# A fused two-block transformer: the second product of gates in the sparse-attention layer moves behind both products of queries

## The reference, cut to what matters

```python
q, kc, vc, ks, vs, kw, vw, gate, z = jnp.split(u @ w_in, points, axis=-1)
q = q.reshape(b, s, G, J, dh) * (dh ** -0.5)
k_cmp = compress(kc, pe_k, w1_k, w2_k)      # 31 compressed positions
v_cmp = compress(vc, pe_v, w1_v, w2_v)
...
s_c = einsum(q, k_cmp) + bias; p_c = softmax(s_c)      # compressed branch
s_s = einsum(q, k_g) + bias;   p_s = softmax(s_s)      # selected branch (all 8 blocks of 8 here)
s_w = einsum(q, k_win) + bias; p_w = softmax(s_w)      # window branch
o = gate[..., 0:1] * o_c + gate[..., 1:2] * o_s + gate[..., 2:3] * o_w
o = o.reshape(b, s, NSA_WIDTH) * jax.nn.silu(z)
return o @ w_out
```

## Time and profile before

| what | value |
|---|---|
| median of three runs | 2103.62 us (2100.56 to 2103.94) |
| the profiled execution | 2101.62 us, of which its span is 2100.3 us |
| PE busy | 2047.3 us, 97% of the span |
| DVE, ACT, POOL busy | 966.2, 776.9, 337.9 us |
| mean granted clock of PE | 0.994 of full speed |

### The profile page before, as it was taken

How to read it: one execution, slowest core, us unless ns; L and a number is a source line. 1 busy time by engine, 2 the same in 40 slices (tenths; PEclk the granted TensorE clock), 3 DMA queues, 4 the chain that set the end, 5 groups by cost and what they waited for, 6 DMA issues and landing times.

```text
span 2100.3 us, 26714 instructions
## 1 busy us (share of the span) xinstructions
PE 2047.3 (97%) x10149; PEld 1658.7 (79%) x10149; DVE 966.2 (46%) x1968; ACT 776.9 (37%) x1548; POOL 337.9 (16%) x501
## 2 busy tenths in 40 slices
PE   7998999999999999999999999999998999999998
PEld 5887887888888886688888888887787888777766
DVE  4438434433354344535534443364435664535445
ACT  4226332222233222323332222242336884434453
POOL 2103110000001120000110000034003674402211
PEclk9999999999999999999999999999998999999999
DMA  5330242333324331133243333325321002323212
GB/s 177 101 100 11 64 121 82 100 97 94 101 71 141 100 95 56 41 100 98 73 122 99 100 91 100 96 86 168 100 79 61 25 29 101 105 79 105 70 48 81
DMA packets 96766, 187.32 MB, mean 89 GB/s; under 512 B 8407, under 2 KB 16639, under 8 KB 96512
## 3 DMA queue, kind: packets, MB, share of 16 engines
q1 hardware_dynamic: 90288, 164.35, 26.1%
q0 software_dynamic: 6352, 21.27, 3.2%
HBM read 181.33 MB, written 4.26 MB: 88 GB/s over the span
## 4 chain that ended last, share of the span: by engine, by line
PE 86%; ACT 5%; DVE 3%; issue 2%; POOL 1%; DMA 1%; SPq 0%; ACTq 0%; DVEq 0%; POOLq 0%
PE bank L754 60%; PE bank L790 8%; PE bank L1262 5%; PE bank L1021 2%; PE bank L1183 1%; PE bank L1160 1%; PE bank L1276 1%; ACT sc L1792 1%; PE bank L826 1%; PE bank L1006 1%; PE bank L1092 1%; PE bank L1299 1%; DVE wl L1963 1%; ACT xn L1786 1%; DMA raw<-in_nsa_w_in 1%
## 5 line engine op out<-in xcount | busy, mean ns | idle before, releaser
L1963 DVE TENSOR_TENSOR wl<-raw,wh 128x1024 fp32r<-128x1024 f32 x306 | 375.1, 1231 | 777.3 <-ACT wh L1379 776.5
L1379 ACT ACTIVATE wh<-raw 128x1024 fp32r<-128x1024 f32 x306 | 321.0, 1053 | 843.9 <-PE bank L754 789.3
L754 PE MATMUL bank<-hTh,wh 128*128 128x512 f32 (+2 forms) x1200 | 467.7, 390 | 3.3 <-ACT kvc L1720 3.1
L754 PE MATMUL bank<-hTl,wh 128*128 128x512 f32 (+2 forms) x1200 | 467.0, 389 | 0.0
L754 PE MATMUL bank<-hTh,wl 128*128 128x512 f32 (+2 forms) x1200 | 466.9, 389 | 0.0
L754 PEld LDWEIGHTS bank<-hTh,wh 128*128 128x128 f32 (+2 forms) x1200 | 223.9, 187 | 52.3 <-ACT kvc L1720 3.5
L754 PEld LDWEIGHTS bank<-hTh,wl 128*128 128x128 f32 (+2 forms) x1200 | 223.9, 187 | 48.2
L754 PEld LDWEIGHTS bank<-hTl,wh 128*128 128x128 f32 (+2 forms) x1200 | 224.0, 187 | 47.9
L754 PE MATMUL bank<-wh,hTh 128*128 128x512 f32 x400 | 156.5, 391 | 0.1
L754 PE MATMUL bank<-wh,hTl 128*128 128x512 f32 x400 | 155.7, 389 | 0.0
L754 PE MATMUL bank<-wl,hTh 128*128 128x512 f32 x400 | 155.6, 389 | 0.0
(11 more groups left out here) (383 smaller groups left out, 3121.0 us busy)
## 6 DMA issues: line engine op xcount, KB each, us to landing
raw<-in_ffn_w_in SPq DMA_DIRECT2D x88, 512.0 KB, 3.7
raw<-in_ret_w_in SPq DMA_DIRECT2D x48, 512.0 KB, 3.8
raw<-in_ffn_w_out SPq DMA_DIRECT2D x44, 512.0 KB, 3.7
raw<-in_diff_w_in SPq DMA_DIRECT2D x32, 512.0 KB, 3.7
raw<-in_fox_w_in SPq DMA_DIRECT2D x24, 512.0 KB, 4.2
raw<-in_nsa_w_in SPq DMA_DIRECT2D x20, 512.0 KB, 3.6
raw<-in_ret_w_out SPq DMA_DIRECT2D x16, 512.0 KB, 3.7
raw<-in_fox_w_out SPq DMA_DIRECT2D x8, 512.0 KB, 3.7
```

The source lines that it names most:

```text
L754: i = pe.do.matmul(dst, x, y, start=first and k == 0 and q == 0, stop=stop)
L1379: act.do.activation(M.hl[n % HL_SLOTS][0][:, 0:m], M.raw[n % RAW_SLOTS][:, 0:m], ACT.Copy).then_inc(*T.up("act_hi", n))
L1963: dve.do.tensor_tensor(wl[:, 0:m], M.raw[n % RAW_SLOTS][:, 0:m], wh[:, 0:m].bitcast(F32), ALU.subtract).then_inc(*T.up("dve_lo", n))
```

## The change

Three things change, all of them orders; no arithmetic is added or removed.

1. The table of chunks, PE, ACT and DVE have the products in the order `nsa q0`, `nsa q4`, `nsa z4`. `HALF_Z4` is the number of the chunk of `nsa z4` with features 256 to 511, the second of its four.
2. The takes of `nsa q4` get one more wait, for the product of chunk `HALF_Z4`, since they write over slices 0 to 3, which `nsa z4` still reads.
3. ACT takes `nsa q0` as before, then calls `act_product(act, T, M, 4)` twice, then takes `nsa q4`, notes the end of the stage, and then takes `nsa z4`. DVE takes `nsa q0`, calls `dve_product(dve, T, M, 4)` twice, and takes `nsa q4`.

```diff
--- before.py
+++ after.py
@@ -115,9 +115,9 @@
     block8("nsa", (1536, 256), (2048, 256))
     chunks.append(("nsa", 0, 8, ((2560, 48),)))
     block8("nsa", (2608, 512))
-    block8("nsa", (3120, 512))
     block8("nsa", (0, 512))
     block8("nsa", (512, 512))
+    block8("nsa", (3120, 512))
     block8("nsao", (0, 512))
     block8("nsao", (512, 512))
     for b in (4, 0, 2, 1, 3, 5, 6, 7):
@@ -128,6 +128,7 @@
 
 
 CHUNKS = weight_chunks()
+HALF_Z4 = CHUNKS.index(("nsa", 256, 2, ((3120, 512),)))
 
 
 
@@ -1120,10 +1121,10 @@
                          start=True, stop=True)
     i.then_inc(*up("pe_cmp", "values"))
     pe.free[b] = [("dve_vcmp", "values")]
-    pe_product(pe, T, M, "nsa z4", "F", 8, h_, ready, 512, dve_frees("act_z", "nsa z4"))
     for base in (0, 4):
         pe_product(pe, T, M, f"nsa q{base}", "F", 8, h_, ready, 512,
                    lambda o: [("act_qhi", base + o), ("dve_qlo", base + o)])
+    pe_product(pe, T, M, "nsa z4", "F", 8, h_, ready, 512, dve_frees("act_z", "nsa z4"))
     T.note("pe", "nsa heads")
 
     def cmp_scores(h):
@@ -1754,6 +1755,8 @@
             hi = M.xn[0][:, b * S:b * S + S]
             act.wait_ge(*at("pe_product", (f"nsa q{base}", o)))
             act.wait_ge(*at("pe_cmp", ("hidden", 1)))
+            if base:
+                act.wait_ge(*at("pe_product", ("chunk", HALF_Z4)))
             if t >= 2:
                 act.wait_ge(*at("act_q", t - 2))
                 act.wait_ge(*at("dve_q", t - 2))
@@ -1773,10 +1776,15 @@
     act.wait_ge(*at("pe_cmp", "keys"))
     act.do.activation(a.kcmp[:, :, 0:31], M.bank[bank["nsa keys"]][:, 0:124].rearrange("p (g c) -> p g c", g=4), ACT.Copy).then_inc(
         *up("act_kcmp", "hi"))
-    act_product(act, T, M, 4, 4, take_z(4))
     act_product(act, T, M, 4, 4, take_q(0))
-    act_product(act, T, M, 4, 4, take_q(4))
+    act_product(act, T, M, 4)
+    act_product(act, T, M, 4)
+    late_q, late_z = take_q(4), take_z(4)
+    for o in range(4):
+        late_q(o)
     T.note("act", "nsa heads")
+    for o in range(4):
+        late_z(o)
     stage_begins(act, T, "nsa heads")
 
     def exp(n):
@@ -2465,6 +2473,8 @@
             r = 64 * (t // 2 % 2)
             hi, lo = (x[:, b * S:b * S + S] for x in M.xn)
             dve.wait_ge(*at("act_qhi", t))
+            if base:
+                dve.wait_ge(*at("pe_product", ("chunk", HALF_Z4)))
             if t >= 2:
                 dve.wait_ge(*at("dve_q", t - 2))
             dve.do.scalar_tensor_tensor(out=lo, in0=M.bank[bank[f"nsa q{base}"][o]][:, :], scalar=0.125, in1=hi, op0=ALU.mult,
@@ -2503,9 +2513,12 @@
     for k in range(4):
         dve.do.tensor_copy(a.vcmp[32 * k:32 * k + 31, k, :, :], M.bank[bank["nsa values"]][0:31, 0:256].rearrange("p (g n) -> p g n", g=4)).then_inc(
             *up("dve_vcmp", "values"))
+    dve_product(dve, T, M, 4, 4, take_q(0))
     dve_product(dve, T, M, 4)
-    dve_product(dve, T, M, 4, 4, take_q(0))
-    dve_product(dve, T, M, 4, 4, take_q(4))
+    dve_product(dve, T, M, 4)
+    late_q = take_q(4)
+    for o in range(4):
+        late_q(o)
     T.note("dve", "nsa heads")
     stage_begins(dve, T, "nsa heads")
```

## The result

The changed kernel takes 2106.3 us (median of 20 runs, 2105.21 to 2109.73) against 2102.95 us before (20 runs, 2100.56 to 2106.78): a ratio of 1.0019, 95% interval 1.0013 to 1.0025. It is slower: by 3.35 us between the medians and by 4.0 us (2.7 to 5.3) by the ratio, which fits the 4.0 us of the sum. The profiled execution has a span of 2106.8 us, 6.5 more than before.

The account below looks back on a forecast made before the run. PE was taken as the bound, except from 1601.85 to 1608.50 us, where ACT leads. Takes +5.10 and work behind them -1.06 gave +4.0 us, put on the 2102.6 median: 2106.6, rounded to 2107 us, range 2103.5 to 2110.5.

Parts of the forecast that it names:

- the 4.0 us of the sum: First exponential of attention on ACT: takes end 5.10 us later, work behind them 1.06 us shorter, so +4.0 us.
- Takes later, not earlier: Takes of `nsa q4` on ACT and DVE: held behind the ninth split, ending on ACT at 1602.60, before 1597.50.
- The bound of 0.2%: Whole kernel time: a difference below 0.2% (4.2 us) can't be told from none; same 0.44, slower 0.50.
- Table load: ACT, ahead of the first exponential: load at 1604.6 right behind the Silus, nothing added; rival drain +1.4 us, chance 0.06.
- DVE 1.0 us ahead of ACT: Before the first exponential: DVE's maximum done by 1603.6, ACT's Silus at 1604.6, so ACT is later by 1.0 us.
- PE's new waits cost nothing: PE at the start of scores, waiting for banks 0 and 3: no cost, 1.5 us to spare, 1 us at most.
- The clock at half on the path, unchanged: PE at the start of attention: slow clock costs as before, taken as 0, between -1.9 and +1.9 us.
- The rival of a late clock: PE at the start of attention: slow part longer by up to 3.8 us, +5 to +6, about 2108.5; chance 0.18.
- The rival in which the clock stays up: PE at the start of attention: clock kept at 2.4 GHz saves 1.9 us, +2.1, 2104.7; chance 0.12.
- Takes under the product, -5.2 us: Rival: takes of `nsa q4` run under `nsa z4`, exponential 3.3 us earlier, clock up 1.9 more, 2097.4; chance 0.05.

Follow-up runs that it names:

- two splits behind: Changed kernel with two of the nine splits moved behind the takes of `nsa q4` on ACT and DVE; 2098.91 us, ratio to before 0.9986.
- the pair alone moved: Kernel before, with only the last split pair ahead of attention moved behind attention on ACT and DVE; 2101.22 us, ratio to before 0.9995.
- the pair at tile 24: Changed kernel with two splits moved behind the takes of `nsa q4`, the last split pair made in attention at tile 24; 2100.3 us, ratio to before 0.9992.
- PE kept busy: Changed kernel, two splits behind the takes, last split pair behind attention, plus ten unread PE matmuls in gaps of attention's first tiles; 2095.11 us, ratio to before 0.9966.
- the repeat: Second run of the unaltered kernel with the last split pair behind attention, as comparison for PE kept busy; 2097.62 us, ratio to before 0.9980.
- the pair behind attention: As the kernel with the pair at tile 24, but the last split pair is made behind the attention loops; 2097.39 us, ratio to before 0.9974.

## Why the prediction was right

- *Takes later, not earlier.* Right, and shown by moving the splits: nine, eight and seven of them ahead of the takes give D 11.87, 7.40 and 4.44. The added wait has no effect in the changed kernel.
- *The sum of +4.0 us.* Measured +4.12 in D, W and A, and 3.35 us between the medians. The products end at 1596.54 and not at 1594.1, because of the two falls of the clock far ahead. Relative to that end every instant is within 0.1 us: split +0.1, take +1.1, Silus +8.5, load +10.6.
- *The bound of 0.2%.* The prediction gave "slower" 0.50 and "same" 0.44 by it. Measured are 0.19% (0.13 to 0.25): the runs don't say on which side of it the change lies, only that it is slower than before.
- *Table load.* It starts 0.02 us behind the last Silu (1605.03 + 2.06 to 1607.11) and the exponential at 1608.41. The drain of about 1.38 us that the Trainium skill ("ScalarE: Activation LUTs", What ACT_TABLE_LOAD costs) adds is not seen here either.
- *DVE 1.0 us ahead of ACT.* Right in kind: the exchange of Silus and takes cost 1.08 us.
- *PE's new waits cost nothing.* Right: scores of tile 2 run from 1606.32 to 1607.05, DVE's maximum for them at 1609.02.
- *The clock at half on the path, unchanged.* Right for this pair of profiles (3.9 us in both), and partly luck: over eleven profiles the stretch behind W was 3.4 to 3.9 us seven times, 6.1 to 6.9 three times, and 0 where PE was kept busy. Half of it is paid each time. The rival of a late clock deserved its 0.18. The rival in which the clock stays up is out: the window from 1598 to 1600 shows 0.63, and the clock is at half until 1619.0.
- *Takes under the product, -5.2 us.* With two splits behind, -3.6 in A: the 3.3 of D were right, the 1.9 for a clock that stays up were not.

## What to carry to other kernels

Before a wait is written for work that may start early, look at what stands ahead of that work in its own queue: here a split that waits for the very end of the product made the earlier wait void. Work that the next stage doesn't need goes to where its engines stand idle (A 157.31 and 156.11 here), not to where they merely have time to spare on average (159.17). And where PE stands, look at the granted clock behind that place: half of the slow time that lies on the path is paid as well, 1.7 to 3.5 us here. Its length did not follow that of the stands: before, PE stood for 4.8 and 1.0 us and 3.9 us of slow time lay on the path; with the pair alone moved it stood for 3.0 and 1.6 us, and 6.9 us did.

## What the runs showed that was not expected

- The stage's length followed one line to 0.4 us in nine of eleven profiles (the exceptions are the pair at tile 24, 3.4 us, and PE kept busy, 0.6 us): last wait for ACT + 145.4 us + half of the time at 1.2 GHz. The 145.4 was set before the profile with PE kept busy and the repeat were taken; that a slow microsecond costs half of one is borne out by the two profiles of one kernel (2.7 us less of it, 1.2 us less in A).
- PE's clock fell with stands of 1.5 us in the kernel with two splits behind, and in the one with the pair behind attention only near 1602.2, 5.7 us after PE's first gap began (at 1596.51). With ten matmuls of 0.22 to 0.23 us each in the gaps, some 2.3 us in all, it did not fall in the one profile taken. The Trainium skill ("TensorE: Matmul & The Clock Gate", Part 1) says that the moment of the rise varies with the run. The two profiles of one kernel agree: the clock rose 14.7 us behind the product in one and 12.6 in the other, after slow stretches of 6.8 and 3.4 us.
